# Gate-matrix stage, group order and selection lookups of a PEER decoder step: subtractions moved between engines, sparse work spread anew, sums by adds of halves

## What is computed

```python
q = (xb @ w_query).reshape(PEER_BLOCK, PEER_HEADS, 2, PEER_HALF)
s = jnp.einsum('bhpd,phnd->bhpn', q, sub_keys).astype(jnp.float32)
top_s, top_i = lax.top_k(s, PEER_TOPK)
cand = top_s[:, :, 0, :, None] + top_s[:, :, 1, None, :]
best_s, best_j = lax.top_k(cand.reshape(PEER_BLOCK, PEER_HEADS, PEER_TOPK * PEER_TOPK), PEER_TOPK)
e1 = jnp.take_along_axis(top_i[:, :, 0, :], best_j // PEER_TOPK, axis=-1)
e2 = jnp.take_along_axis(top_i[:, :, 1, :], best_j % PEER_TOPK, axis=-1)
eid = e1 * PEER_NKEYS + e2
gate = jax.nn.softmax(best_s, axis=-1)
u_sel = expert_u[eid]
act = jax.nn.gelu(jnp.einsum('bd,bhkd->bhk', xb, u_sel).astype(jnp.float32), approximate=False)
v_sel = expert_v[eid]
return jnp.einsum('bhk,bhkd->bd', (gate * act).astype(xb.dtype), v_sel)
```

## Time and profile before

| what | us |
|---|---|
| median of 3 executions (3801.97 to 3807.18) | 3806.78 |
| the profiled execution, its own time | 3811.23 |
| its span in the profile | 3809.5 |
| selection, from DVE's first tile to its last eviction | 1289.9 to 1733.4 |
| gate-matrix stage | 1733.4 to 2095.4 |
| groups | 2099 to 3780 |
| share of the span: PE / DVE / ACT / POOL | 91% / 69% / 27% / 28% |

### The profile page before, as it was taken

How to read it: one execution, slowest core, us unless ns; L and a number is a source line. 1 busy time by engine, 2 the same in 40 slices (tenths; PEclk the granted TensorE clock), 3 DMA queues, 4 the chain that set the end, 5 groups by cost and what they waited for, 6 DMA issues and landing times.

```text
span 3809.5 us, 57302 instructions
## 1 busy us (share of the span) xinstructions
PE 3467.4 (91%) x21552; PEld 3385.4 (89%) x21552; DVE 2623.9 (69%) x4889; ACT 1017.8 (27%) x1345; POOL 1063.9 (28%) x809
## 2 busy tenths in 40 slices
PE   6989999899998999886888799999999999999997
PEld 6989999699998999885777789999999999999996
DVE  5553434223443499997666788888888888888886
ACT  5732222111322232222333222222222222222222
POOL 0000000000000233221111545555455555544551
PEclk8999999699999999997888999999999999999998
DMA  2111111111322233224655989888888888888983
GB/s 100 39 36 37 35 44 44 50 44 45 135 84 73 93 116 106 88 92 127 190 180 180 347 309 323 297 301 307 295 312 322 317 300 308 309 307 311 323 307 106
DMA packets 304485, 699.11 MB, mean 184 GB/s; under 512 B 23872, under 2 KB 124224, under 8 KB 303328
## 3 DMA queue, kind: packets, MB, share of 16 engines
q0 software_dynamic: 98736, 363.50, 26.3%
q1 hardware_dynamic: 104112, 276.89, 21.4%
q10 hardware_dynamic: 101504, 56.89, 4.9%
HBM read 604.96 MB, written 92.22 MB: 183 GB/s over the span
## 4 chain that ended last, share of the span: by engine, by line
PE 64%; DVE 22%; DMA 6%; issue 4%; ACT 2%; POOL 1%; DVEq 1%; ACTq 0%; SPq 0%; PEldq 0%; POOLq 0%
PE PS L1420 21%; PE PS L358 15%; PE PS L1135 6%; PE PS L1403 5%; PE PS L1164 5%; PE PS L1343 5%; DMA SLOT<-rows_u,EID 4%; DVE XLF L1927 3%; PE PS L1382 3%; DVE SLOT L1918 2%; POOL WL L674 1%; PE PS L373 1%; DVE VL L1911 1%; DVE besti L1775 1%; DVE sc L1766 1%
## 5 line engine op out<-in xcount | busy, mean ns | idle before, releaser
L1420 PE MATMUL PS<-AH,VH 128*128 128x368 f32 x2048 | 523.0, 337 | 90.7 <-DVE VL L1911 76.9
L1420 PE MATMUL PS<-AH,VL 128*128 128x368 f32 x2048 | 517.5, 334 | 0.0
L1420 PE MATMUL PS<-AL,VH 128*128 128x368 f32 x2048 | 516.9, 334 | 0.0
L1420 PEld LDWEIGHTS PS<-AH,VH 128*128 128x128 f32 x2048 | 368.8, 191 | 102.1 <-DVE VL L1911 87.0
L704 POOL DMA_INDIRECT SLOT<-rows_u,EID x256 | 334.3, 1306 | 384.2 <-DVE XLF L1927 304.0
L704 POOL DMA_INDIRECT SLOT<-rows_v,EID x256 | 362.9, 1417 | 247.3 <-DVE SLOT L1918 214.9
L1420 PEld LDWEIGHTS PS<-AL,VH 128*128 128x128 f32 x2048 | 371.5, 191 | 0.0
L1420 PEld LDWEIGHTS PS<-AH,VL 128*128 128x128 f32 x2048 | 371.2, 191 | 0.0
L1998 DVE TENSOR_TENSOR HID<-HID,PS 128x736 f32<-128x736 f32 x256 | 235.4, 919 | 177.4 <-PE PS L1420 162.8
L1343 PE MATMUL PS<-XH,WH 128*128 128x368 f32 x1024 | 278.6, 352 | 80.2 <-POOL WL L674 80.2
L674 POOL TENSOR_TENSOR WL<-RAW,WH 128x1024 fp32r<-128x1024 f32 x64 | 172.2, 2692 | 628.5 <-ACT WH L947 628.5
(11 more groups left out here) (327 smaller groups left out, 6741.8 us busy)
## 6 DMA issues: line engine op xcount, KB each, us to landing
RAW<-experts_u SPq DMA_DIRECT2D x128, 512.0 KB, 3.7
VRAW<-experts_v SPq DMA_DIRECT2D x256, 256.0 KB
gate_matrices<-stg ACTq DMA_DIRECT2D x22, 2048.0 KB, 8.8
GW<-gate_matrices SPq DMA_DIRECT2D x96, 384.0 KB
RAW<-weights SPq DMA_DIRECT2D x69, 512.0 KB, 3.5
activations<-AS SPq DMA_DIRECT2D x64, 368.0 KB, 2.5
AS<-activations SPq DMA_DIRECT2D x64, 368.0 KB
GW<-gate_matrices SPq DMA_DIRECT2D x32, 320.0 KB
```

Source lines behind the costliest of these rows:

```text
L1420: mm = pe.matmul(PS[:, 4 + 2 * (d % 2) + t, 0:CH], w[:, d % 2, c * P:c * P + P], x[:, c, t * CH:t * CH + CH], start=(c == 0 and n == 0), s ...
```

## The change

Four parts. (1) Two dense blocks move from the gate-matrix stage into the selection: SEL_E has a 5 in place of a 4 for the sixth and the ninth tile, so E0 is 46 and 18 blocks are left. (2) In the gate-matrix stage the subtractions of the 17 blocks behind the first move from POOL to DVE's queue, each three steps after the end of the block two before it, and ACT splits a block's weights right after the block two before it has ended, one block earlier than till now. (3) In the groups PE takes (0,3) ahead of (1,2), and of the sparse instructions two fewer stand between the last late set and the first HID addition; they stand in the loop over d, at d = 3 and d = 6. (4) In the lookups every table is fp16 and laid out as [64 pairs of winners, 16, 2], so that the two elements of a pair are neighbours; each tensor_reduce is replaced by four additions of halves (8, 4, 2 and 1 of 16 left), with a drain between; one further copy (second) lays out the second keys' indices.

```diff
-SEL_E = (5, 5, 5, 5, 5, 4, 5, 4, 4)
+SEL_E = (5, 5, 5, 5, 5, 5, 5, 4, 5)
...
+        def e_end(m):
+            return min(s for s in range(NSTEP) if e_steps(s)[1] >= len(STEPS) * (m - E0 + 1))
...
@@ POOL
-            for n in range(E0 + 1, NE):
-                e_low(n, n % 2)
...
@@ ACT, gate-matrix stage
+            e_split((E0 + 1) % 2, E0 + 2, 16 * ((E0 + 1) // 2 + 1))
             for s in range(NSTEP):
...
-                    e_block(m, m % 2, 16 * (m // 2 + 1), m + 1 < NE)
+                    e_block(m, m % 2, 16 * (m // 2 + 1), False)
+                    if m + 2 < NE:
+                        e_split(m % 2, m + 3, 16 * ((m + 2) // 2 + 1))
...
@@ PE, groups
-                order = [(d, c) for cs in (range(GE - 1), (GE - 1,)) for d in range(2) for c in cs]
+                order = [(0, 0), (0, 1), (0, 2), (1, 0), (1, 1), (0, 3), (1, 2), (1, 3)]
...
@@ DVE, sel_dve
+                dve.tensor_copy(second[:, :, :, :], f2[:, :, 1, :].unsqueeze(3).broadcast_to([w, HP, TOPK, 2]))
...
+                def places(x):
+                    return x[:, :].rearrange("p (a b) -> p a b", b=2).unsqueeze(2).broadcast_to([w, PAIRS // 2, TOPK, 2])
+                def names(x):
+                    return x[:, :, :].unsqueeze(1).broadcast_to([w, PAIRS // 2, TOPK, 2])
...
+                def fold(out):
+                    src = pick
+                    for to in folds:
+                        dve.drain()
+                        v = src[:, :, :, :].rearrange("p a (j e) b -> p (a j) e b", e=2)
+                        dve.tensor_tensor(to[:, :, :, :].rearrange("p a j b -> p (a j) b"), v[:, :, 0, :], v[:, :, 1, :], ALU.add)
+                        src = to
+                    dve.drain()
+                    dve.tensor_tensor(out[:, :].rearrange("p (a b) -> p a b", b=2), src[:, :, 0, :], src[:, :, 1, :], ALU.add)
...
-                dve.tensor_tensor(r(hot), each(r(topf)), row(const("start16", w)), ALU.is_ge)
+                dve.tensor_tensor(hot[:, :, :, :], places(topf), names(startb), ALU.is_ge)
                 dve.drain()
-                dve.tensor_tensor(r(pick), r(hot), over(r(delta)), ALU.mult)
+                dve.tensor_tensor(by_head(pick), by_head(hot), values(delta), ALU.mult)
+                fold(e1)
+                dve.tensor_tensor(pick[:, :, :, :], hot[:, :, :, :], names(dstart), ALU.mult)
+                fold(firstf)
                 dve.drain()
-                dve.tensor_reduce(e1v, r(pick), AX.X, ALU.add)
+                dve.tensor_tensor(topf[:, :], topf[:, :], firstf[:, :], ALU.subtract)
                 dve.drain()
-                dve.tensor_tensor(r(pick), r(hot), row(r(dstart)), ALU.mult)
+                dve.tensor_tensor(hot[:, :, :, :], places(topf), names(iota_b), ALU.is_equal)
                 dve.drain()
-                dve.tensor_reduce(e2v, r(pick), AX.X, ALU.add)
...
-                dve.tensor_tensor(r(pick), r(hot), over(f2[:, :, 1, :]), ALU.mult)
-                dve.drain()
-                dve.tensor_reduce(e2v, r(pick), AX.X, ALU.add)
+                dve.tensor_tensor(by_head(pick), by_head(hot), values(second), ALU.mult)
+                fold(e2)
...
@@ DVE, gate-matrix stage, at the end of step s
+                for m in range(E0 + 1, NE):
+                    if s == (e_end(m - 2) + 3 if m > E0 + 1 else 2):
+                        dve.wait_ge(e_lo, m)
+                        dve.wait_ge(e_hi, m + 1)
+                        dve.tensor_tensor(WL[:, m % 2, :], RAW[:, m % 2, :], WH[:, m % 2, :].bitcast(F32),
+                                          ALU.subtract).then_inc(e_lo, 1)
...
@@ DVE, group_dve
-                    for j in range(early[0], early[0] + n):
+                    for j in range(early[0], min(early[0] + n, SPR)):
...
-                    between(2 if h == 0 else 3)
+                    between(2 if h == 0 else SPR if first else 1)
...
-                    some((3 if d < 4 else 2) if first else 2 if d in (2, 4) else 1)
+                    some((3 if d < 4 else 2) if first else 2 if d in (2, 3, 4) else 1 if d < 7 else 0)
```

More of the change, by code:

```diff
@@ L219, in program @@
         sc2 = at(sel0 + 8192, "sc2", [P, 2 * HP, NKEYS])
-        hot = at(sel0 + 16384, "hot", [P, HP, TOPK, TOPK], BF16)
-        pick = at(sel0 + 20480, "pick", [P, HP, TOPK, TOPK], BF16)
+        hot = at(sel0 + 16384, "hot", [P, PAIRS // 2, TOPK, 2], F16)
+        pick = at(sel0 + 20480, "pick", [P, PAIRS // 2, TOPK, 2], F16)
         cand = at(sel0 + 24576, "cand", [P, HP, NCAND])
@@ L232, in program @@
         besti = small_at("besti", [P, 2 * HP, TOPK], U32)
-        bestf = small_at("bestf", [P, 2 * HP, TOPK], BF16)
-        delta = small_at("delta", [P, HP, TOPK], BF16)
+        bestf = small_at("bestf", [P, 2 * HP, TOPK], F16)
+        delta = small_at("delta", [P, HP, TOPK, 2], F16)
+        second = small_at("second", [P, HP, TOPK, 2], F16)
+        folds = [small_at(f"fold{n}", [P, PAIRS // 2, n, 2], F16) for n in (8, 4, 2)]
         top = small_at("top", [P, HP, TOPK])
         topi = small_at("topi", [P, HP, TOPK], U32)
-        topf = small_at("topf", [P, HP, TOPK])
+        topf = small_at("topf", [P, HP * TOPK], F16)
+        firstf = small_at("firstf", [P, HP * TOPK], F16)
         e1 = small_at("e1", [P, PAIRS])
@@ L252, in program @@
         as0 = r2 + 68096
-        assert o[0] <= r2 + 55808 and oh0 + 18432 <= r2 + 51712
+        assert o[0] <= r2 + 64000 and oh0 + 18432 <= r2 + 51712
         AS = at(as0, "AS", [P, EARLY, ND])
@@ L1805, in sel_dve @@
+                dve.tensor_copy(second[:, :, :, :], f2[:, :, 1, :].unsqueeze(3).broadcast_to([w, HP, TOPK, 2]))
                 dve.drain()
-                dve.tensor_copy(r(topf), r(topi))
+                dve.tensor_copy(topf[:, :], topi[:, :, :].rearrange("p h k -> p (h k)"))
                 dve.drain()
[L1809 to L1815, removed]
@@ L1826, in sel_dve @@
                 dve.drain()
-                dve.tensor_tensor(r(pick), r(hot), row(r(dstart)), ALU.mult)
+                dve.tensor_tensor(hot[:, :, :, :], places(topf), names(iota_b), ALU.is_equal)
                 dve.drain()
-                dve.tensor_reduce(e2v, r(pick), AX.X, ALU.add)
-                dve.drain()
-                dve.tensor_tensor(r(topf), r(topf), e2v, ALU.subtract)
-                dve.drain()
-                dve.tensor_tensor(r(hot), each(r(topf)), row(const("iota16", w)), ALU.is_equal)
@@ L1866, in _ @@
             dve.wait_ge(iota_set, 1)
-            dve.tensor_tensor(dstart[:, 1:TOPK], const("start16")[:, 1:TOPK], const("start16")[:, 0:TOPK - 1], ALU.subtract)
-            dve.tensor_copy(dstart[:, 0:1], const("start16")[:, 0:1])
+            starts = const("start16").unsqueeze(2)
+            dve.tensor_copy(startb[:, :, :], starts.broadcast_to([P, TOPK, 2]))
+            dve.tensor_tensor(dstart[:, 1:TOPK, :], starts[:, 1:TOPK].broadcast_to([P, TOPK - 1, 2]),
+                              starts[:, 0:TOPK - 1].broadcast_to([P, TOPK - 1, 2]), ALU.subtract)
+            dve.tensor_copy(dstart[:, 0:1, :], starts[:, 0:1].broadcast_to([P, 1, 2]))
             dve.drain().then_inc(sel_done, 1)
@@ L1954, in between @@
                         return some(n)
-                    for j in range(early[0], early[0] + n):
+                    for j in range(early[0], min(early[0] + n, SPR)):
                         sp_u(0, j, j)
-                    early[0] += n
+                        early[0] = j + 1
                 def gates():
```

23 lines of the change are left out of this document (12 added, 11 removed).

## The result

The changed kernel takes 3598.97 us (median of 4 executions, 3593.56 to 3605.75) against 3806.98 us for the kernel before on the same chip. The ratio is 0.9457, with a 95% interval from 0.9436 to 0.9478: 208 us less. Forecast were 3614, with 3585 to 3658 as the range and 3590 to 3640 for the likeliest case alone.

The account below looks back on a forecast made before the run. Bounds: DVE in the selection, waits for POOL's subtraction in the gate-matrix stage, PE with waits for DVE's VL subtraction in the groups. 3811.2 - 112 - 72 - 9 = 3618, median 4.4 lower: 3614 us, range 3585 to 3658.

Parts of the forecast that it names:

- the likeliest case: Whole kernel: the forecast itself, 3614 us, chance 0.56, with 3590 to 3640 us as its own range.
- DVE's sum of 241: Gate-matrix stage: 92 steps of 2.41 us are 222 us, 17 added subtractions 19 us, sum 241.
- the load behind the later release: Gate-matrix stage: weight loads wait for DVE's subtraction; one over 14 us stalls DVE and PE. Total over 3807, chance 0.04.
- The 9 us for filling: Gate-matrix stage: 9 us added for filling, the last step and small waits behind each subtraction, giving 250 us.
- that rival: Groups: gathers take over as two move into the product stretch; half the wait stays, 50.4 a group, 3653 us. Chance 0.16.
- Its base of 48.9: Groups: PE's own work per group, 34.6 - 1.8 us in the products and 16.1 in the activations.
- The rival of the missing double rate: Lookups: additions of halves with gaps miss the double rate, costing 28 us in 27 sums: 3642 us. Chance 0.09.
- the strict reading of the rule on gaps: Lookups: the skill's double-rate mode asks for 16-bit elements with a step of one; taken strictly that forbids the gaps.
- two of the five subtractions of a tile fall: Lookups: two POOL subtractions a tile hold DVE up 2.0 us each, 4.0 in place of 2.1; net saving 9 us.
- The 14 us at a pace of 8.07: Selection: argument that lookups of 14 us hold only two POOL subtractions, which come at a pace of 8.07.
- The prediction's own argument against this part: Lookups: a two-input tensor_tensor locks the shared ports, a tensor_reduce never; keeping reductions leaves 2.1 us of hold-ups a tile.
- the selection grows: Selection: four subtractions a tile caught, lookup longer by 1.1 us; selection + 9, total 3632 us. Chance 0.15.

Follow-up runs that it names:

- another kernel: The changed kernel with the 17 subtractions of the gate-matrix stage back on POOL, ACT's early split kept: 3630.56 us, ratio 0.9523.

## Why the prediction was right, and where its sizes were off

- **What bounds each stage** was read rightly: DVE the selection, POOL's late subtraction the gate-matrix stage, DVE's VL subtraction the groups. The runs with one part each show it for the last two, the run without POOL's reading for the first, where the selection fell by 41 us.
- **The gate-matrix stage**: 250 forecast, 248.8 measured (248.7 with this part alone), against 362 and, in the cut used here, 365.7. DVE's sum of 241 is what the rows add up to. PE was put at 231 and was busy for 240.1, nearer to the bound than forecast, but hardly shows. The store, landing in 10.3 us where the earlier trace rows had 8.8, ends only 4.1 us of ACT's waits, and the load behind the later release never ended a wait of PE. The 9 us for filling are 7.8, nearly all of them behind DVE's last one-hots and not in waits behind each subtraction. The two blocks, costed at nothing in the selection, cost nothing there.
- **The groups**: 72 forecast, 90.6 measured, outside the 45 to 78. The mechanism held: both halves were needed, no wait is left, no gather took over (DVE waits for gathered rows 6.1 us in all, in six waits of the first groups), so that rival falls. Mis-sized was the group, 49.1 for 48.51. Its base of 48.9 came from a group with its wait in it, of which only the 1.8 shown were taken off; the run with the sparse instructions alone shows that a wait delays PE by 0.24 more than its idle time (0.84 for 0.60). That is over half of the 0.4 by which the base was too long; for the rest I have no row. The 0.2 a group left for gathers was not needed either. The first two groups gave another 1.8 and 3.2 us, where the forecast counted them like the rest.
- **The lookups' own time**: 13.7 forecast, 13.48 measured; 16.6 for the old, 16.60 measured. The rival of the missing double rate falls with the 0.69 us, and so does the strict reading of the rule on gaps.
- **The hold-ups** are the step that failed, "two of the five subtractions of a tile fall" into the lookups: it is 5.2 us a tile, some 2.6 of them, and not 4.0. So the gain was nothing clear of scatter (0 us alone, 2 in the profiles) and not 9. Why so many are caught is in part argued. The 14 us at a pace of 8.07 were read from undisturbed lookups; with the hold-ups a lookup lasts 17 to 20 us, which at that pace gives 2.1 to 2.5, and in the tile shown POOL's subtractions come 7.7 and 6.8 apart. The prediction's own argument against this part, that a reduction is not held up, was the better guide: it put lookups with reductions at 2.1 us a tile, and they measured 1.5. The rival "the selection grows" had the right mechanism and is not refuted: the profiled selection is 2.0 shorter, and the same code took 447.0 in another kernel, over the 443 that the prediction named as its sign of being wrong. It named four caught subtractions for a lookup longer by 1.1, where by its own 2.0 each that is the price of three.
- **The sum**: the stages give 117 + 91 + 2 = 209.5 where 193 were forecast: the groups gave 19 more, the gate-matrix stage 5 more, the lookups 7 less. That the total lies in the likeliest case's own range, though the groups' saving doesn't lie in theirs, is in part luck, as the misses have both signs. The rest of the profiled execution's 216.1 is the 6.6 us ahead of the selection. The medians differ by 208.0, as the three parts alone do to within 1 us.

## What to carry to other kernels

A gain worked out for one engine's instructions is none while another engine's hold them up: here adds that are each 0.5 us shorter than a reduction left the kernel 22 us slower than with the reductions, because the other engine's work had hidden under them. Where one wait has two causes in a queue, look for both halves of the cure: PE's order gave 7 us, the moved work 71, both 94. And read a wait between pipelined matmuls from start to start, since the idle time shown leaves out their overlap.

## What was unexpected of the hardware

- Five POOL subtractions of 2.4 us took from 11.75 to 14.97 beside DVE instructions of two inputs that follow each other without a gap, and four of them ended only once DVE stood still. In the changed kernel's selection, where a drain stands between most of the lookups' instructions, the longest is 3.3 us, and there it is DVE that waits. That the drains hand the ports over fits both, but no run took only the drains away: it stays argued.
- An instruction with one input can be held up too: a CAST of 128x128 took 2.44 us for 0.23 beside a subtraction of POOL (first tile of the changed kernel), and 0.98 beside POOL's memset.
- The reduction over the strided view of the pairs takes 2285 to 2289 ns in all 27 cases, as the one over the contiguous table.
- The short waits of the groups cost no clock: behind 0.60 and 1.57 us the second pair is at 0.50 and the granted clock 1.00, behind 3.56 it is at 0.81. In the changed kernel's groups the granted clock is 1.00 over 1418 us, and one group is like the next to 0.01 us.
